# Block products' weights 32 bytes into longer slots, and a gap that moves the tensors behind it

## The chip, the core and the metric

One core of one Trainium2 chip runs the whole kernel as one program. The metric is device time of one execution in microseconds: the median over runs of the kernel. Before the change it is 1858.59 us in three runs (1858.54 to 1861.07).

## The reference

A trunk of two layers works on two requests of 256 tokens each, with shared weights, in float32. The tokens of both requests stand side by side: 512 columns of 1024 features. Each layer computes

```python
h = x + 0.5 * _swiglu(_rmsnorm(x, ffn1_norm[l]), ffn1_wg[l], ffn1_wu[l], ffn1_wd[l])
u = _rmsnorm(h, mix_norm[l])
p = u @ w_in[l]
ret = _retention(...)      # 4 heads of 128, forward and backward
dif = _diff_attn(...)      # 4 heads, differential attention with a relative bias
h = h + jnp.concatenate([ret, dif], axis=-1) @ w_out[l]
h = h + 0.5 * _swiglu(_rmsnorm(h, ffn2_norm[l]), ffn2_wg[l], ffn2_wu[l], ffn2_wd[l])
x = _rmsnorm(h, final_norm[l])
```

with `_swiglu(x, wg, wu, wd) = (silu(x @ wg) * (x @ wu)) @ wd` and 2816 hidden features. So there are four feed-forward networks (FFNs), two per layer, and they hold most of the multiplications.

## The kernel before, in words

Activations lie in SBUF with features on the 128 partitions and tokens along the free dimension. A weight matrix comes as units of 8 tiles of 128x128. A unit is loaded into a raw buffer (`raw`, `raw_x`), and split into a high and a low part of type float32r: ScalarE (ACT) writes the high part into `w_hi`, GpSimd (POOL) or VectorE (DVE) the difference into `w_lo`. Activations are split in the same way (`hg_hi`/`hg_lo`, `a_hi`/`a_lo`, `mix_*`, `s14_*`, `s2_*`). A product of two tiles is three matmuls that accumulate in one PSUM bank: weight high with activation high (L742), weight high with activation low (L743), weight low with activation high (L744), in the helper `three`. The program has a weight load for each of these matmuls.

There are six weight slots. Slots 0 to 3 are `w_hi[:, s]` and `w_lo[:, s]`; slots 4 and 5 are in further tensors `w_hi_x`, `w_lo_x`, which exist only in the FFNs. Each slot holds 8 tiles of 128 floats in a partition, 4096 bytes. `w_tiles(s, n, at_)` gives `n` tiles of a slot from tile `at_` on.

Whole units use a slot with 512 moving columns: all of attention's projections and output products (slots 0 to 3), two gate and up pairs at the start of an FFN (`CLASSIC_SLOT`), and the down products of the last chunk (`DOWN_SLOT`, which takes slots 4 and 5 too).

The rest of an FFN goes in 28 blocks. A block treats two units as a 2x2 matrix of half units, against the 2x2 of (halves of the features or hidden tiles) by (the two requests), and needs seven half-size products instead of eight, after Strassen and Winograd. So one block is 7 products of 4 tiles by 3 matmuls, 84 matmuls with 256 moving columns each. Block "t" makes a gate and up tile (20 of the 28), block "d" two down products (8 of them). Some products read `hg` or `a` directly, the others mixtures of two quarters: `mix_*` (mixtures of `hg`) in "t", `s14_*` and `s2_*` (gated sums) in "d". Even blocks use slots 0, 1, 2, odd ones 3, 4, 5 (`FAST_SLOTS`). TensorE's order in a block is p1, p6, p2, p5, p7, p4, p3; the two d blocks that open a chunk's down products have an order of their own. p1 and p2 use the first slot, p5 and p7 the second, p6, p4 and p3 the third. In "t", p1, p2, p4 and p3 read `hg` and p6, p5, p7 read `mix`; in "d", p1, p2, p7, p4 read `a` and p6, p5, p3 read `s14`, `s2`.

The order of all this is written out by hand for each engine, with semaphores: in `ffn` and `block_slot` of each engine. PE waits for a product's weights (POOL at L645, L663, L670, DVE at L1774) and for VectorE to have taken former products out of PSUM (`u` at L1800 and L1810 among them). Raw units are loaded by the SP queue.

SBUF tensors are placed one behind the other in a partition in the order of their declaration, each at the next multiple of 32 bytes. In the kernel before, `h` (at byte 1152) up to `blocks_r` all start at multiples of 64 bytes, since their sizes are. Behind them come small ones (`pr`, `eps`, ..., `lam`), and these leave off so that `raw_x` starts at byte 148320, 32 above a multiple of 64. Every further tensor has a multiple of 64 bytes again, so `raw_x`, `w_hi_x`, `w_lo_x`, `mix_*`, `up`, `s14_*` and `s2_*` start 32 above one. The tensors of attention (`decay`, `s1`, ..., `dkq`, `rkq`, `v`, `soft`) share that place in memory after the FFN's are given back, and start 32 above one too. All offsets within these tensors that a matmul reads from are multiples of 512 bytes.

Of the kernel before, what the change touches and what calls it, by code (L numbers as in the profile page):

```python
# [30 lines left out]
F32R = mybir.dt.float32r  # L31
# [4 lines left out]
P = 128  # L36
# [24 lines left out]
FAST = NF - CLASSIC  # L61
KH = KD // 2


# [131 lines left out]
def build(nc, x, w_gu, w_dn, w_p, w_o, par, lam_vec, table, one_hot, cossin, rel, ident_in, centre_in, y):  # L196
    with ExitStack() as ctx:
# [15 lines left out]
        raw = sb("raw", [P, RAW * UT * P])  # L213
        w_hi = sb("w_hi", [P, SLOTS, UT, P], F32R)
        w_lo = sb("w_lo", [P, SLOTS, UT, P], F32R)
        acc = sb("acc", [P, T])
# [19 lines left out]
        lg = sb("lg", [P, 8, 2 * HEADS])  # L236
        lam = sb("lam", [P, 6])


        with ExitStack() as ffn_only:  # L240
            def sb_ffn(name, shape, dt=F32):
                return ffn_only.enter_context(nc.sbuf_tensor(name, shape, dt))

            raw_x = sb_ffn("raw_x", [P, RAW * UT * P])
            w_hi_x = sb_ffn("w_hi_x", [P, 2, UT, P], F32R)
            w_lo_x = sb_ffn("w_lo_x", [P, 2, UT, P], F32R)
            mix_hi = sb_ffn("mix_hi", [P, 3, KH, SEQ], F32R)
# [365 lines left out]
        def _(pool):  # L613
# [45 lines left out]
            def lo_differences(l, f, b):  # L659
                pool.wait_ge(t13_hi, at(t13_hi, l, index(f, b) + 1))  # L660
                hi, lo_ = w_tiles(FAST_SLOTS[b % 2][1])
                both = raw_of(b)[:, :].rearrange("p (a b) -> p a b", a=2)[:, :, 0:KH * P]
                pool.tensor_tensor(columns(lo_).rearrange("p (a b) -> p a b", a=2), both,  # L663
                                   columns(hi).rearrange("p (a b) -> p a b", a=2).bitcast(F32),
                                   ALU.subtract).then_inc(t13_lo, 1)

            def lo_b22(l, f, b):
                pool.wait_ge(b22_hi, at(b22_hi, l, index(f, b) + 1))
                hi, lo_ = w_tiles(FAST_SLOTS[b % 2][2], KH, KH)
                pool.tensor_tensor(columns(lo_), raw_block(b, 1, 1), columns(hi).bitcast(F32),  # L670
                                   ALU.subtract).then_inc(b22_lo, 1)
# [66 lines left out]
        def _(pe):  # L738
            def three(out, w, m_hi, m_lo, first, last):

                hi, lo_ = w_tiles(w[0], 1, w[1])
                pe.matmul(out, hi[:, 0, :], m_hi, start=first, stop=False)  # L742
                pe.matmul(out, hi[:, 0, :], m_lo, start=False, stop=False)  # L743
                return pe.matmul(out, lo_[:, 0, :], m_hi, start=False, stop=last)  # L744
# [11 lines left out]
            def fresh_product(l, out, u, s, m_hi, m_lo):  # L756

                pe.wait_ge(hi_done, at(hi_done, l, u + 1))
                for k in range(UT):
                    pe.matmul(out, w_hi[:, s, k, :], m_hi[:, k, :], start=k == 0, stop=False)  # L760
                    pe.matmul(out, w_hi[:, s, k, :], m_lo[:, k, :], start=False, stop=False)
                pe.wait_ge(lo_done, at(lo_done, l, u + 1))
                for k in range(UT):
                    last = pe.matmul(out, w_lo[:, s, k, :], m_hi[:, k, :], start=False, stop=k == UT - 1)
                return last

            def first_two(l, outs, u, n0, done, between=None):
# [7 lines left out]
                for s in range(2):  # L775
                    pe.wait_ge(hi_done, at(hi_done, l, u + s + 1))
                    for k in range(EARLY):
                        if s == 0:
                            tile_hi(k)
                        pe.matmul(outs[s], w_hi[:, s, k, :], hg_hi[:, k, :], start=k == 0, stop=False)  # L780
                for s in range(2):
                    pe.wait_ge(lo_done, at(lo_done, l, u + s + 1))
                    for k in range(EARLY):
                        pe.matmul(outs[s], w_lo[:, s, k, :], hg_hi[:, k, :], start=False, stop=False)  # L784
                for s in range(2):
                    for k in range(EARLY):
                        if s == 0:
                            tile(k)
                        pe.matmul(outs[s], w_hi[:, s, k, :], hg_lo[:, k, :], start=False, stop=False)  # L789
                for s in range(2):  # L790
# [8 lines left out]
            def first_units():  # L799
# [3 lines left out]
                def high(s, k):  # L803
                    if s == 0:
                        pe.wait_ge(hg_hi_done, at(hg_hi_done, 0, k + 1))
                    pe.matmul(outs[s], w_hi[:, s, k, :], hg_hi[:, k, :], start=k == 0, stop=False)

                def moving_low(s, k):
                    if s == 0:
                        pe.wait_ge(hg_ready, at(hg_ready, 0, k + 1))  # L810
                    pe.matmul(outs[s], w_hi[:, s, k, :], hg_lo[:, k, :], start=False, stop=False)

                def weight_low(s, k, last=False):
                    return pe.matmul(outs[s], w_lo[:, s, k, :], hg_hi[:, k, :], start=False, stop=last)

# [20 lines left out]
                pe.wait_ge(hg_ready, at(hg_ready, 0, KD))  # L836
                pe.matmul(outs[0], w_hi[:, 0, KD - 1, :], hg_lo[:, KD - 1, :], start=False, stop=True).then_inc(gu_done, 1)
                moving_low(1, KD - 1)
# [352 lines left out]
        def _(act):  # L1191
# [27 lines left out]
            def hi_gate(l, f, b):  # L1219
                m = index(f, b)  # L1220
                raw_wait(l, ("t", m, 0))
                slot_free(l, f, b, 0, 4 if after_first_pair(b) else 2)
                act.activation(columns(w_tiles(FAST_SLOTS[b % 2][0])[0]), raw_tiles(RAW_AT["t", m, 0], UT),  # L1223
                               ACT.Copy).then_inc(g_hi, 1)

            def hi_differences(l, f, b):
                act.wait_ge(t13_done, at(t13_done, l, index(f, b) + 1))
                slot_free(l, f, b, 1, 5 if after_first_pair(b) else 7)
                both = raw_of(b)[:, :].rearrange("p (a b) -> p a b", a=2)[:, :, 0:KH * P]
                hi = columns(w_tiles(FAST_SLOTS[b % 2][1])[0]).rearrange("p (a b) -> p a b", a=2)  # L1230
                act.activation(hi, both, ACT.Copy).then_inc(t13_hi, 1)  # L1231

            def hi_b22(l, f, b):
                raw_wait(l, ("t", index(f, b), 1))
                slot_free(l, f, b, 2, 3)
                hi, _ = w_tiles(FAST_SLOTS[b % 2][2], KH, KH)
                act.activation(columns(hi), raw_block(b, 1, 1), ACT.Copy).then_inc(b22_hi, 1)
# [12 lines left out]
            def hi_t2(l, f, b):  # L1250
                act.wait_ge(t2_done, at(t2_done, l, index(f, b) + 1))
                slot_free(l, f, b, 2, 6 if after_first_pair(b) else 4)
                act.activation(columns(w_tiles(FAST_SLOTS[b % 2][2], KH)[0]), t_sum, ACT.Copy).then_inc(x_hi, 1)

            def hi_t4(l, f, b):
# [3 lines left out]
                act.wait_ge(p_done[q], at(p_done[q], l, m + 1))  # L1259
                act.activation(columns(w_tiles(t4_slot(b), KH)[0]), t_sum, ACT.Copy).then_inc(x_hi, 1)  # L1260

# [397 lines left out]
        def _(dve):  # L1659
# [111 lines left out]
            def lo_t(l, f, b, which):  # L1771
                dve.wait_ge(x_hi, at(x_hi, l, 2 * index(f, b) + which + 1))
                hi, lo_ = w_tiles(t4_slot(b) if which else FAST_SLOTS[b % 2][2], KH)
                dve.tensor_tensor(columns(lo_), t_sum, columns(hi).bitcast(F32), ALU.subtract).then_inc(x_lo, 1)  # L1774
# [558 lines left out]
```

## Time and profile before

| | |
|---|---|
| median of 3 runs | 1858.59 us |
| lowest, highest | 1858.54, 1861.07 us |
| span of the profiled execution | 1859.7 us |
| mean granted TensorE clock | 0.998 of full |
| PE busy, PEld busy | 1840.7 us, 1705.5 us |
| DVE, ACT, POOL busy | 1373.1, 1016.8, 1347.7 us |
| matmuls | 12668 |

The page gives the span of the profiled execution (from its first to its last instruction) and no time around it. Busy time of an engine is the time in which at least one of its instructions runs. For PE this hides how fast matmuls follow each other: one takes some 280 ns at 256 columns from its start to its end, but the next starts long before that. So for PE the distance between starts is read from the timeline or from counts in a stretch.

### The profile page before, as it was taken

How to read it: one execution, taken by the hardware profiler on the slowest of the kernel's cores; microseconds unless marked ns; L12 is line 12 of the kernel's file. 1: busy time of each engine (PE TensorE's matmuls, PEld its weight loads, DVE VectorE, ACT ScalarE, POOL GpSimd, SP SyncE). 2: the span in 40 equal slices, each digit the busy share in tenths (PEclk: the TensorE clock that was granted, in tenths of full speed). 3: DMA queues.
4: the chain of work that ended last, by engine and by line, in shares of the span. 5: the costliest groups of instructions: out<-in, count | busy, mean ns of one | idle time of the engine just before them, and what ended most of it. 6: DMA issues, size and time to landing. Idle time of an engine off the chain costs nothing. (4 is left out here: it accounts for less than half of the span.)

```text
span 1859.7 us, 33422 instructions
## 1 busy us (share of the span) xinstructions
PE 1840.7 (99%) x12668; PEld 1705.5 (92%) x12668; DVE 1373.1 (74%) x2396; ACT 1016.8 (55%) x1763; POOL 1347.7 (72%) x878
## 2 busy tenths in 40 slices
PE   8999999999999999999999999999999999999997
PEld 7999999887888999999889999998778889999995
DVE  6878887556755887887688888766577478878773
ACT  7655555456435655555575465555564266555452
POOL 5988897565445898988479998856544268988972
PEclk9999999999999999999999999999999999999999
DMA  3433233232223233323233333223222133323331
GB/s 138 154 112 126 96 126 114 77 103 70 69 68 113 73 110 114 106 100 108 75 113 137 100 106 114 105 78 114 79 68 73 53 113 115 106 100 114 105 106 63
DMA packets 55308, 186.71 MB, mean 100 GB/s; under 512 B 6472, under 2 KB 8264, under 8 KB 55148
## 3 DMA queue, kind: packets, MB, share of 16 engines
q1 hardware_dynamic: 53424, 181.61, 29.0%
q10 hardware_dynamic: 1724, 2.96, 0.5%
q8 instruction: 101, 1.65, 0.4%
q14 instruction: 59, 0.48, 0.1%
HBM read 182.44 MB, written 3.15 MB: 100 GB/s over the span
## 5 line engine op out<-in xcount | busy, mean ns | idle before, releaser
L742 PE MATMUL bank<-hg_hi,w_hi 128*128 128x256 f32 (+1 forms) x1396 | 445.2, 319 | 0.0
L743 PE MATMUL bank<-hg_lo,w_hi 128*128 128x256 f32 (+1 forms) x1396 | 441.4, 316 | 0.0
L744 PE MATMUL bank<-hg_hi,w_lo 128*128 128x256 f32 (+1 forms) x1396 | 441.2, 316 | 0.0
L636 POOL TENSOR_TENSOR w_lo<-raw,w_hi 128x512 fp32r<-128x512 f32 (+1 forms) x192 | 256.9, 1361 | 225.3 <-ACT w_hi L1206 225.2
L742 PEld LDWEIGHTS bank<-hg_hi,w_hi 128*128 128x128 f32 x1396 | 264.9, 190 | 19.9 <-issue 2.6
L744 PEld LDWEIGHTS bank<-hg_hi,w_lo 128*128 128x128 f32 x1396 | 265.1, 190 | 17.6
L743 PEld LDWEIGHTS bank<-hg_lo,w_hi 128*128 128x128 f32 x1396 | 265.1, 190 | 16.8
L1286 ACT ACTIVATE bank<-bank 128x512 f32<-128x512 f32 x88 | 51.1, 581 | 251.5 <-DVE bank L1831 251.5
L1206 ACT ACTIVATE w_hi<-raw 128x1024 fp32r<-128x1024 f32 (+1 forms) x96 | 98.0, 1025 | 120.2 <-PE bank L744 95.7
L663 POOL TENSOR_TENSOR w_lo<-raw_x,w_hi 128x1024 fp32r<-128x1024 f32 x56 | 134.9, 2410 | 26.3 <-ACT w_hi L1231 26.3
L645 POOL TENSOR_TENSOR w_lo<-raw_x,w_hi 128x1024 fp32r<-128x1024 f32 x56 | 136.1, 2430 | 17.0 <-ACT w_hi L1223 17.0
L663 POOL TENSOR_TENSOR w_lo_x<-raw,w_hi_x 128x1024 fp32r<-128x1024 f32 x56 | 135.0, 2410 | 14.1 <-ACT w_hi_x L1231 14.1
L645 POOL TENSOR_TENSOR w_lo<-raw,w_hi 128x1024 fp32r<-128x1024 f32 x56 | 136.5, 2438 | 2.7 <-ACT w_hi L1223 2.7
L742 PE MATMUL bank<-mix_hi,w_hi_x 128*128 128x256 f32 x480 | 135.5, 282 | 1.6 <-DVE u L1800 1.6
L742 PE MATMUL bank<-mix_hi,w_hi 128*128 128x256 f32 x480 | 135.2, 282 | 0.8 <-POOL w_lo L663 0.5
L744 PE MATMUL bank<-mix_hi,w_lo_x 128*128 128x256 f32 x480 | 135.3, 282 | 0.0
L743 PE MATMUL bank<-mix_lo,w_hi 128*128 128x256 f32 x480 | 135.1, 281 | 0.0
L743 PE MATMUL bank<-mix_lo,w_hi_x 128*128 128x256 f32 x480 | 134.9, 281 | 0.0
L744 PE MATMUL bank<-mix_hi,w_lo 128*128 128x256 f32 x480 | 134.5, 280 | 0.0
L742 PE MATMUL bank<-a_hi,w_hi 128*128 128x256 f32 (+1 forms) x448 | 134.0, 299 | 0.0
L743 PE MATMUL bank<-a_lo,w_hi 128*128 128x256 f32 (+1 forms) x448 | 133.5, 298 | 0.0
L744 PE MATMUL bank<-a_hi,w_lo 128*128 128x256 f32 (+1 forms) x448 | 133.5, 298 | 0.0
(342 smaller groups left out, 5831.5 us busy)
## 6 DMA issues: line engine op xcount, KB each, us to landing
raw<-in_w_gu SPq DMA_DIRECT2D x96, 512.0 KB, 4.0
raw_x<-in_w_gu SPq DMA_DIRECT2D x80, 512.0 KB, 4.2
raw<-in_w_p SPq DMA_DIRECT2D x56, 512.0 KB, 3.2
raw_x<-in_w_dn SPq DMA_DIRECT2D x32, 512.0 KB, 4.2
raw<-in_w_dn SPq DMA_DIRECT2D x32, 512.0 KB, 4.2
raw<-in_w_o SPq DMA_DIRECT2D x16, 512.0 KB, 3.3
raw_x<-in_w_dn SPq DMA_DIRECT2D x16, 384.0 KB, 4.0
raw<-in_w_dn SPq DMA_DIRECT2D x16, 384.0 KB, 3.4
```

The costliest lines, as they stand in the source:

```text
L636: ins = pool.tensor_tensor(columns(lo_[:, part, :]), source[:, part.start * P:part.stop * P], columns(hi[:, part, :]).bitcast(F32), ALU.su ...
L645: pool.tensor_tensor(columns(lo_), raw_tiles(RAW_AT["t", m, 0], UT), columns(hi).bitcast(F32), ALU.subtract).then_inc(g_lo, 1)
L663: pool.tensor_tensor(columns(lo_).rearrange("p (a b) -> p a b", a=2), both, columns(hi).rearrange("p (a b) -> p a b", a=2).bitcast(F32), A ...
L742: pe.matmul(out, hi[:, 0, :], m_hi, start=first, stop=False)
L743: pe.matmul(out, hi[:, 0, :], m_lo, start=False, stop=False)
L744: return pe.matmul(out, lo_[:, 0, :], m_hi, start=False, stop=last)
L1206: act.activation(columns(hi), raw_tiles(RAW_AT["e", e], TILES_OF[e]), ACT.Copy).then_inc(hi_done, 1)
L1286: act.activation(gated, gated, ACT.Silu).then_inc(silu_done, 1)
```

## The change: the diff and what it does

Each slot becomes a flat row of `SLOT` = 8 x 128 + 16 floats, 4160 bytes. Block products write and read their weights 8 floats (32 bytes) into the slot, through the new `block_tiles`; whole units still use it from its start, through `w_tiles`. A tensor `gap` of 8 floats (32 bytes), which nothing reads or writes, is declared behind `lam`. By the placing rule above, `raw_x` then starts at byte 148864, a multiple of 64, and all tensors behind it move likewise. No instruction is added or taken away, and none changes its shape.

```diff
+BLOCK_AT = 8
+SLOT = UT * P + 2 * BLOCK_AT
+GAP = 8
...
-        w_hi = sb("w_hi", [P, SLOTS, UT, P], F32R)
-        w_lo = sb("w_lo", [P, SLOTS, UT, P], F32R)
+        w_hi = sb("w_hi", [P, SLOTS, SLOT], F32R)
+        w_lo = sb("w_lo", [P, SLOTS, SLOT], F32R)
...
         lam = sb("lam", [P, 6])
+        sb("gap", [P, GAP])
...
-            w_hi_x = sb_ffn("w_hi_x", [P, 2, UT, P], F32R)
-            w_lo_x = sb_ffn("w_lo_x", [P, 2, UT, P], F32R)
+            w_hi_x = sb_ffn("w_hi_x", [P, 2, SLOT], F32R)
+            w_lo_x = sb_ffn("w_lo_x", [P, 2, SLOT], F32R)
...
-        def w_tiles(s, n=UT, at_=0):
+        def w_tiles(s, n=UT, at_=0, shift=0):
             hi, lo = (w_hi[:, s], w_lo[:, s]) if s < SLOTS else (w_hi_x[:, s - SLOTS], w_lo_x[:, s - SLOTS])
-            return hi[:, at_:at_ + n, :], lo[:, at_:at_ + n, :]
+            part = slice(shift + at_ * P, shift + (at_ + n) * P)
+            return hi[:, part].rearrange("p (a b) -> p a b", b=P), lo[:, part].rearrange("p (a b) -> p a b", b=P)
+
+        def block_tiles(s, n=UT, at_=0):
+            return w_tiles(s, n, at_, BLOCK_AT)
...
-                hi, lo_ = w_tiles(FAST_SLOTS[b % 2][0])
+                hi, lo_ = block_tiles(FAST_SLOTS[b % 2][0])
...
-            def three(out, w, m_hi, m_lo, first, last):
-                hi, lo_ = w_tiles(w[0], 1, w[1])
+            def three(out, w, m_hi, m_lo, first, last, tiles=w_tiles):
+                hi, lo_ = tiles(w[0], 1, w[1])
...
-                    last = three(prod[q] if out is None else out, (w, KH * half + k), m_hi[:, k, :], m_lo[:, k, :], k == 0, k == KH - 1)
+                    last = three(prod[q] if out is None else out, (w, KH * half + k), m_hi[:, k, :], m_lo[:, k, :],
+                                 k == 0, k == KH - 1, block_tiles)
```

The places that write block weights (`lo_gate`, `lo_differences`, `lo_b22` on POOL, `hi_gate`, `hi_differences`, `hi_b22`, `hi_t2`, `hi_t4` on ACT, `lo_t` on DVE) take `block_tiles` for `w_tiles` in the same way, and direct uses of `w_hi[:, s, k, :]` on PE become `w_hi[:, s, k_part(k)]` with the same addresses in the slot.

## Rows read from the trace of the kernel before

**Rows 1.** The page's first lines: busy us, share of the span, instructions.

```profile
span 1859.7 us, 33422 instructions
PE 1840.7 (99%) x12668; PEld 1705.5 (92%) x12668; DVE 1373.1 (74%) x2396; ACT 1016.8 (55%) x1763; POOL 1347.7 (72%) x878
```

**Rows 2.** Table by windows, stretches of block products: window, length, busy us, clock, DMA, GB/s.

```profile
core 0: us, PE busy (x) PEld busy (x) DVE busy (x) ACT busy (x) POOL busy (x), PEclk, DMA share, GB/s
...
660.00:880.00 220.00, 220.00 (x1852) 220.00 (x1852) 177.40 (x332) 120.00 (x200) 196.41 (x119) 1.00 0.32 108
...
1580.00:1790.00 210.00, 210.00 (x1769) 210.00 (x1768) 169.59 (x318) 115.29 (x191) 187.01 (x113) 1.00 0.31 106
```

**Rows 3.** Timeline of PE, t blocks 12 and 13: start us, duration us, instruction.

```profile
741.53 0.28 PE L742 MATMUL bank<-mix_hi,w_hi 128*128 128x256 f32 x1
...
742.95 0.28 PE L742 MATMUL bank<-mix_hi,w_hi 128*128 128x256 f32 x1
...
745.80 0.28 PE L742 MATMUL bank<-hg_hi,w_hi 128*128 128x256 f32 x1
...
747.24 0.28 PE L742 MATMUL bank<-hg_hi,w_hi 128*128 128x256 f32 x1
...
752.94 0.28 PE L742 MATMUL bank<-mix_hi,w_hi_x 128*128 128x256 f32 x1
...
754.38 0.28 PE L742 MATMUL bank<-hg_hi,w_hi_x 128*128 128x256 f32 x1
...
754.74 0.28 PE L742 MATMUL bank<-hg_hi,w_hi_x 128*128 128x256 f32 x1
...
757.21 0.28 PE L742 MATMUL bank<-hg_hi,w_hi 128*128 128x256 f32 x1
```

**Rows 4.** Timeline of PE, d block 9: first matmuls of p7, p4 and p3.

```profile
713.00 0.28 PE L742 MATMUL bank<-a_hi,w_hi_x 128*128 128x256 f32 x1
...
714.42 0.28 PE L742 MATMUL bank<-a_hi,w_hi_x 128*128 128x256 f32 x1
...
715.83 0.28 PE L742 MATMUL bank<-s_h,w_hi_x 128*128 128x256 f32 x1
```

**Rows 5.** Timeline of PE, last down products with 512 columns, slots 3, then 4.

```profile
908.45 0.39 PE L742 MATMUL pair<-a_hi,w_hi 128*128 128x512 f32 x1
...
913.21 0.39 PE L742 MATMUL pair<-a_hi,w_hi 128*128 128x512 f32 x1
...
913.90 0.39 PE L742 MATMUL pair<-a_hi,w_hi_x 128*128 128x512 f32 x1
...
921.60 0.40 PE L742 MATMUL pair<-a_hi,w_hi_x 128*128 128x512 f32 x1
```

**Rows 6.** Groups by line and form, PE, 512 columns from slots 4 and 5.

```profile
L742 PE MATMUL pair<-a_hi,w_hi_x 128*128 128x512 f32 x72 | 28.4, 395 | 0.0
...
L742 PE MATMUL pair<-hg_hi,w_hi_x 128*128 128x512 f32 x32 | 12.7, 398 | 0.0
```

**Rows 7.** The page's groups: POOL's low parts; busy us, mean ns, idle before.

```profile
L663 POOL TENSOR_TENSOR w_lo<-raw_x,w_hi 128x1024 fp32r<-128x1024 f32 x56 | 134.9, 2410 | 26.3 <-ACT w_hi L1231 26.3
...
L663 POOL TENSOR_TENSOR w_lo_x<-raw,w_hi_x 128x1024 fp32r<-128x1024 f32 x56 | 135.0, 2410 | 14.1 <-ACT w_hi_x L1231 14.1
```

**Rows 8.** Timeline of POOL and DVE, low parts for block 13.

```profile
744.76 2.42 POOL L663 TENSOR_TENSOR w_lo_x<-raw,w_hi_x 128x1024 fp32r<-128x1024 f32 x1
...
750.98 0.69 DVE L1774 TENSOR_TENSOR w_lo_x<-bank,w_hi_x 128x512 fp32r<-128x512 f32 x1 [0.32 <-ACT w_hi_x L1260]
```

**Rows 9.** PE's waits, longest in total first: us, times, longest us.

```profile
PE bank L742 <- DVE u L1800: 2.4, 3, 1.1
PE bank L806 <- ACT hg_hi L1631: 2.3, 1, 2.3
```

**Rows 10.** Instructions of lines 854 and 868: duration ns min/median/max, first, last.

```profile
L854 PE MATMUL bank<-s_h,ones_r x6: 397/397/501, 363.7 to 1521.0; 128*128 128x512 f32 x6
...
L868 PE MATMUL bank<-a_hi,blocks_r x16: 389/389/390, 385.9 to 1373.9; 128*128 128x512 f32 x16
```

More of the change, by code:

```diff
@@ L660, in lo_differences @@
                 pool.wait_ge(t13_hi, at(t13_hi, l, index(f, b) + 1))
-                hi, lo_ = w_tiles(FAST_SLOTS[b % 2][1])
+                hi, lo_ = block_tiles(FAST_SLOTS[b % 2][1])
                 both = raw_of(b)[:, :].rearrange("p (a b) -> p a b", a=2)[:, :, 0:KH * P]
@@ L668, in lo_b22 @@
                 pool.wait_ge(b22_hi, at(b22_hi, l, index(f, b) + 1))
-                hi, lo_ = w_tiles(FAST_SLOTS[b % 2][2], KH, KH)
+                hi, lo_ = block_tiles(FAST_SLOTS[b % 2][2], KH, KH)
                 pool.tensor_tensor(columns(lo_), raw_block(b, 1, 1), columns(hi).bitcast(F32),
@@ L738, in _, with k_part @@
         def _(pe):
-            def three(out, w, m_hi, m_lo, first, last):
-                hi, lo_ = w_tiles(w[0], 1, w[1])
+            def k_part(k):
+                return slice(k * P, (k + 1) * P)
+            def three(out, w, m_hi, m_lo, first, last, tiles=w_tiles):
+                hi, lo_ = tiles(w[0], 1, w[1])
                 pe.matmul(out, hi[:, 0, :], m_hi, start=first, stop=False)
@@ L759, in fresh_product @@
                 for k in range(UT):
-                    pe.matmul(out, w_hi[:, s, k, :], m_hi[:, k, :], start=k == 0, stop=False)
-                    pe.matmul(out, w_hi[:, s, k, :], m_lo[:, k, :], start=False, stop=False)
+                    pe.matmul(out, w_hi[:, s, k_part(k)], m_hi[:, k, :], start=k == 0, stop=False)
+                    pe.matmul(out, w_hi[:, s, k_part(k)], m_lo[:, k, :], start=False, stop=False)
                 pe.wait_ge(lo_done, at(lo_done, l, u + 1))
                 for k in range(UT):
-                    last = pe.matmul(out, w_lo[:, s, k, :], m_hi[:, k, :], start=False, stop=k == UT - 1)
+                    last = pe.matmul(out, w_lo[:, s, k_part(k)], m_hi[:, k, :], start=False, stop=k == UT - 1)
                 return last
@@ L779, in first_two @@
                             tile_hi(k)
-                        pe.matmul(outs[s], w_hi[:, s, k, :], hg_hi[:, k, :], start=k == 0, stop=False)
+                        pe.matmul(outs[s], w_hi[:, s, k_part(k)], hg_hi[:, k, :], start=k == 0, stop=False)
                 for s in range(2):
@@ L783, in first_two @@
                     for k in range(EARLY):
-                        pe.matmul(outs[s], w_lo[:, s, k, :], hg_hi[:, k, :], start=False, stop=False)
+                        pe.matmul(outs[s], w_lo[:, s, k_part(k)], hg_hi[:, k, :], start=False, stop=False)
                 for s in range(2):
@@ L788, in first_two @@
                             tile(k)
-                        pe.matmul(outs[s], w_hi[:, s, k, :], hg_lo[:, k, :], start=False, stop=False)
+                        pe.matmul(outs[s], w_hi[:, s, k_part(k)], hg_lo[:, k, :], start=False, stop=False)
                 for s in range(2):
@@ L805, in high @@
                         pe.wait_ge(hg_hi_done, at(hg_hi_done, 0, k + 1))
-                    pe.matmul(outs[s], w_hi[:, s, k, :], hg_hi[:, k, :], start=k == 0, stop=False)
+                    pe.matmul(outs[s], w_hi[:, s, k_part(k)], hg_hi[:, k, :], start=k == 0, stop=False)
                 def moving_low(s, k):
@@ L810, in moving_low @@
                         pe.wait_ge(hg_ready, at(hg_ready, 0, k + 1))
-                    pe.matmul(outs[s], w_hi[:, s, k, :], hg_lo[:, k, :], start=False, stop=False)
+                    pe.matmul(outs[s], w_hi[:, s, k_part(k)], hg_lo[:, k, :], start=False, stop=False)
                 def weight_low(s, k, last=False):
-                    return pe.matmul(outs[s], w_lo[:, s, k, :], hg_hi[:, k, :], start=False, stop=last)
+                    return pe.matmul(outs[s], w_lo[:, s, k_part(k)], hg_hi[:, k, :], start=False, stop=last)
                 pe.wait_ge(hi_done, at(hi_done, 0, 1))
@@ L836, in first_units @@
                 pe.wait_ge(hg_ready, at(hg_ready, 0, KD))
-                pe.matmul(outs[0], w_hi[:, 0, KD - 1, :], hg_lo[:, KD - 1, :], start=False, stop=True).then_inc(gu_done, 1)
+                pe.matmul(outs[0], w_hi[:, 0, k_part(KD - 1)], hg_lo[:, KD - 1, :], start=False, stop=True).then_inc(gu_done, 1)
                 moving_low(1, KD - 1)
@@ L1222, in hi_gate @@
                 slot_free(l, f, b, 0, 4 if after_first_pair(b) else 2)
-                act.activation(columns(w_tiles(FAST_SLOTS[b % 2][0])[0]), raw_tiles(RAW_AT["t", m, 0], UT),
+                act.activation(columns(block_tiles(FAST_SLOTS[b % 2][0])[0]), raw_tiles(RAW_AT["t", m, 0], UT),
                                ACT.Copy).then_inc(g_hi, 1)
@@ L1229, in hi_differences @@
                 both = raw_of(b)[:, :].rearrange("p (a b) -> p a b", a=2)[:, :, 0:KH * P]
-                hi = columns(w_tiles(FAST_SLOTS[b % 2][1])[0]).rearrange("p (a b) -> p a b", a=2)
+                hi = columns(block_tiles(FAST_SLOTS[b % 2][1])[0]).rearrange("p (a b) -> p a b", a=2)
                 act.activation(hi, both, ACT.Copy).then_inc(t13_hi, 1)
@@ L1235, in hi_b22 @@
                 slot_free(l, f, b, 2, 3)
-                hi, _ = w_tiles(FAST_SLOTS[b % 2][2], KH, KH)
+                hi, _ = block_tiles(FAST_SLOTS[b % 2][2], KH, KH)
                 act.activation(columns(hi), raw_block(b, 1, 1), ACT.Copy).then_inc(b22_hi, 1)
@@ L1252, in hi_t2 @@
                 slot_free(l, f, b, 2, 6 if after_first_pair(b) else 4)
-                act.activation(columns(w_tiles(FAST_SLOTS[b % 2][2], KH)[0]), t_sum, ACT.Copy).then_inc(x_hi, 1)
+                act.activation(columns(block_tiles(FAST_SLOTS[b % 2][2], KH)[0]), t_sum, ACT.Copy).then_inc(x_hi, 1)
             def hi_t4(l, f, b):
@@ L1259, in hi_t4 @@
                 act.wait_ge(p_done[q], at(p_done[q], l, m + 1))
-                act.activation(columns(w_tiles(t4_slot(b), KH)[0]), t_sum, ACT.Copy).then_inc(x_hi, 1)
+                act.activation(columns(block_tiles(t4_slot(b), KH)[0]), t_sum, ACT.Copy).then_inc(x_hi, 1)
             def copy_p1(l, f, b):
@@ L1772, in lo_t @@
                 dve.wait_ge(x_hi, at(x_hi, l, 2 * index(f, b) + which + 1))
-                hi, lo_ = w_tiles(t4_slot(b) if which else FAST_SLOTS[b % 2][2], KH)
+                hi, lo_ = block_tiles(t4_slot(b) if which else FAST_SLOTS[b % 2][2], KH)
                 dve.tensor_tensor(columns(lo_), t_sum, columns(hi).bitcast(F32), ALU.subtract).then_inc(x_lo, 1)
```

## The prediction

> **What bounds the kernel now.** I began with the page's first part: TensorE (PE) is busy for 99% of the span, the weight loads (PEld) beside it for 92%, POOL and VectorE for about 72 to 74% [rows 1]. The table by windows then shows what PE does in the stages of block products. In two stretches of 220 and 210 us it is busy without a gap, and it starts 1852 and 1769 matmuls in them [rows 2]. That is 220/1852 = 118.8 ns from one start to the next, and 210/1769 = 118.7 ns. (A matmul's own duration, 0.28 us, is latency; they overlap, so the distance of starts is what costs.) There are 4 FFNs x 28 blocks x 7 products x 12 = 9408 such matmuls, each with 256 moving columns and its own weight load: 1118 us of the 1859.7. Everything else in these stretches is hidden as long as it keeps up. So the question is whether the change alters the distance of starts.
>
> The change moves data and adds no instruction; the operations keep their shapes. Only addresses within a partition move. Before it, every tensor from `h` to `blocks_r`, with `w_hi` and `w_lo` (slots 0 to 3), starts at a multiple of 64 bytes; everything behind `lam` (`raw_x`, slots 4 and 5, the mixtures `mix_*`, the gated sums `s14_*`, `s2_*`) starts 32 bytes above one. The trace of before thus already holds all four pairings of moving operand (M) and weights (W), named by their distance above a multiple of 64. I took them from the timeline as distances between the first matmuls of successive products; a product has 12.
> - M 0, W 0 (`hg` with slot 2): 747.24 - 745.80 = 1.44 us, 120.0 ns each [rows 3].
> - M 32, W 32 (`mix` with slot 4): 754.38 - 752.94 = 1.44 us, 120.0 ns [rows 3].
> - M 32, W 0 (`mix` with slot 1): 742.95 - 741.53 = 1.42 us, 118.3 ns [rows 3].
> - M 0, W 32 (`hg` with slot 5): 21 matmuls from 754.74 to 757.21, 2.47 us, 117.6 ns [rows 3].
>
> Could it be the product's place or its PSUM bank? The product that starts at 752.94 is the fifth of an odd block; the same step four blocks earlier, in a block of down products, with `a` (M 0) for `mix` (M 32) and the same slot and bank, takes 714.42 - 713.00 = 1.42 us where the one with `mix` took 1.44, and the next one 715.83 - 714.42 = 1.41 [rows 3, 4]. So equal phases cost 120.0 ns, and unequal ones about 2 ns less.
>
> With 512 columns it is the other way round. At M 0, W 0, 21 matmuls take 913.21 - 908.45 = 4.76 us, 226.7 ns each; at M 0, W 32, 33 take 921.60 - 913.90 = 7.70 us, 233.3 ns [rows 5].
>
> **The change part by part.** *Block weights at +8 elements, slots lengthened by 64 bytes, a gap of 32 bytes behind `lam`.* A slot is then 4160 = 65 x 64 bytes, so every slot starts at a multiple of 64 and every block product's weights 32 above one. The gap brings `raw_x` and all behind it from 32 to 0. All 9408 block matmuls become M 0, W 32. At 117.6 ns they gain 118.8 - 117.6 = 1.2 ns each, 11.3 us.
> One thing isn't in the trace: slots 0, 2 and 4 put the block weights 32 above a multiple of 128, slots 1, 3 and 5 96 above; the pairing read above had 96 (slots 4 and 5 of before). If 128 bytes matter, the nearest row for the other half is M 32, W 0 with its 118.3 ns (`mix` stands 96 above a multiple of 128, so the weights lie 32 beyond it). Its ends, from the rows of both widths: 117.6 at best, 120.0 plus the 6.6 ns of the 512-column case at worst. I take between 117.6 and 118.3 for that half, the values nearest to it: half of the matmuls, 4704, gain 1.2 ns and the others about 0.9: 5.6 + 4.2 = 9.8 us.
>
> *Slots 4 and 5 for whole units.* The last down products and one of the opening units use them with 512 columns: 3 x (72 + 32) = 312 matmuls [rows 6], which go from 233.3 to 226.7 ns: 2.1 us gained.
>
> *Attention.* Its tensors that share the place behind `lam` go from 32 to 0 together; its projections (slots 0 to 3, `hg`) stay M 0, W 0. Those of slots 1 and 3 come to stand 64 above a multiple of 128, which no row shows; the ends are 226.7 and 233.3 ns. I take 226.7, since all that these rows show goes by 32 against 64.
>
> *ScalarE, VectorE, POOL, DMA.* They write and read the moved tensors in the same shapes. POOL takes 2410 ns for the weights' low part whether it goes from a tensor 32 above to one at 0 or from 0 to 32 [rows 7]. I cost this at nothing.
>
> *What is late next.* The gain holds only where PE is ahead of nobody. POOL has 196.4 of 220 us busy, VectorE 177.4 [rows 2]; with a block shorter by 1% POOL comes to some 90%. The weights are early: in the block read above POOL begins slot 4's low part at 744.76, for 2.42 us, so it is ready at 747.18, and PE uses it from 751.52 (12 matmuls before 752.94, M 32, W 32); VectorE's low part of slot 5 is ready at 751.67 for 754.38 [rows 3, 8]. Covers of 2.7 us and more against 0.1 us a block. But where PE already waits, what it saves ahead of the wait is lost. PE's list of waits has few: 2.4 us in 3 waits for VectorE's `u` (L1800) [rows 9]. They stand in the first two blocks of the first FFN and at the first paired down products of layer 1's first FFN, where VectorE has extra work. What is lost is the saving of the blocks before: about two blocks in each of four FFNs (4 x 2 x 84 x 1.2 ns = 0.8 us) and six more in that one (0.6 us), 1.4 us in all.
>
> **Sum**: -9.8 - 2.1 + 1.4 = -10.5 us. The profiled execution has a span of 1859.7 us, 1.1 above the median of 1858.6 and within the three runs (1858.5 to 1861.1); nothing is shown of what lies around it, so I take the difference from the median: 1848.1, rounded to 1848.0.
>
> **Rivals.**
> 1. *Not the phase, but the place* (the change does nothing to the rate). In the trace of before, "32 above" and "behind `lam`" are the same tensors. If the 2 ns come from operands on two sides of a border in SBUF, the changed kernel keeps every pairing: 1858.6. Against it: `ones_r` with `s2` (M 32) takes 397 ns, its neighbour `blocks_r` with `a` (M 0) 389 at the same 512 columns [rows 10], which phase explains as it stands; a border would have to lie exactly at `lam`. The Trainium skill, page "SBUF — State Buffer", section "Who interferes with whom", would give this result too: it has two independent read ports for PE, moving operand and weights, and says that PE never waits on anyone. By that rule addresses of one could not slow the other, and 1858.6 would stand. The rows at 120.0 and 117.6 ns for one shape disagree with it.
> 2. *The phase counts in 128 bytes, without a gain at 32.* Slots 0, 2, 4 then go at 120.0 (+1.2 on 4704, 5.6 us lost), the others gain 5.6, slots 4 and 5 at 512 columns 2.1: 1856.5 or a little more. For it: only one residue was seen with M 0. Against: M 32, W 0 has the same distance and is fast.
> 3. *The feeders hold it back.* If VectorE's chain through `u` binds in every block rather than in a few, half of the gain goes: 1853. For it: the waits on L1800. Against: the covers above.
> 4. *Slower: misaligned weights cost at 256 columns what they cost at 512.* Place: block products from slots 0, 2 and 4, at 32 above a multiple of 128. Price: 6.6 ns on 4704 matmuls, 31 us, less 5.6 and 2.1 gained elsewhere: 1882. It decides from the first block on. It needs the unseen residue to act like 512 columns although slots 4 and 5 with the same form gain.
>
> **How the numbers follow.** Forecast 0.74, feeders 0.06, place 0.07, 128 bytes without gain 0.07, slower 0.06. The forecast's own range is 1844 (all at 117.6, 118.8 - 117.6 on 9408 and 2.1, nothing lost: -13.4, to 1845.2, with 1 us of spread between runs) to 1851 (all of the unseen half at 118.3 or worse and 3 us lost in waits). Stretched to the cases of rivals 2 and 3 it ends at 1857, which leaves out rival 1 and 4. About 0.2%, 3.7 us, is what a measurement can tell from no change: faster than that 0.74 + 0.06 = 0.80, within it 0.14, slower 0.06.
>
> **What would show it.** In the timeline of after, each product of 12 takes 1.41 to 1.42 us whatever it reads, none 1.44; a block 9.88 to 9.91 instead of 9.98; the two window rows give about 117.7 ns a matmul. Down products from slots 4 and 5 go at 226.7. POOL's and VectorE's durations stay. If even blocks' products from slots 0 and 2 differ from those of slot 1, the 128-byte question is answered. The prediction is wrong if 1.44 us remains with M 0, W 32, or if PE's waits grow by several us.

## The result: slightly slower, and the profile after

| | before | after |
|---|---|---|
| median, us | 1858.54 | 1862.87 |
| lowest to highest | 1858.38 to 1861.18 | 1862.66 to 1864.19 |
| ratio to before, 95% interval | | 1.0021 [1.0014, 1.0027] |
| span of the traced execution, us | 1859.7 | 1862.4 |
| the four block stretches, first to last matmul start, us | 1124.2 | 1120.7 |
| all the rest of the span, us | 735.5 | 741.7 |
| of the rest: ahead of the first block, us | 36.4 | 34.9 |
| of the rest: behind the first block's start, us | 699.1 | 706.8 |
| mean distance of starts within blocks (distances under 150 ns), ns | 118.87 | 118.39 |

The forecast was 1848.0, faster; the kernel became 4.3 us slower (13 runs each). An execution's time lies 1.8 us above its span, so the traced execution of before is one of 1861.4 us, at the top of its runs, and that of after one of 1864.2. The traces therefore differ by 2.7 us where the medians differ by 4.3. The lines of the table below the span are worked out from the starts in the timeline: a block stretch is one FFN's 28 blocks, 2352 matmuls.

Most of the missing 1.6 us lie ahead of the first block, which starts at 36.36 us in the trace of before and at 34.93 in that of after (at 33.4 to 34.5 in the traces of the seven whole kernels further down). PE waits there for its first activations, 2.3 us before [rows 9] and 1.6 after. In the trace of before the granted clock was also lower for a while: 0.86 and 0.72 of full in two windows, 0.50 (the lower level, 1.2 GHz) between 11 and 14 us, while it was 1.00 in those windows of after. Before, then after, columns of [rows 2]:

```profile
8.00:12.00 4.00, 2.46 (x11) 2.07 (x11) 3.49 (x4) 4.00 (x7) 1.63 (x2) 0.86 1.02 358
12.00:16.00 4.00, 4.00 (x16) 3.31 (x15) 4.00 (x6) 4.00 (x7) 2.22 (x2) 0.72 0.18 58
...
8.00:12.00 4.00, 2.53 (x14) 2.16 (x15) 3.54 (x4) 4.00 (x8) 1.56 (x2) 1.00 1.01 365
12.00:16.00 4.00, 4.00 (x20) 3.28 (x19) 4.00 (x6) 4.00 (x7) 2.28 (x2) 1.00 0.14 48
```

So the traces are best compared from the first block on: there the difference is 4.2 us, as between the medians.

The blocks did gain, 3.5 us. The rest behind the first block's start lost 7.7. Both show in rows. The page's first lines of after (answering to [rows 1]):

```profile
span 1862.4 us, 33422 instructions
...
PE 1844.1 (99%) x12668; PEld 1702.3 (91%) x12668; DVE 1380.0 (74%) x2396; ACT 1016.8 (55%) x1763; POOL 1345.9 (72%) x878
```

The table by windows of after, the two stretches of [rows 2], same columns:

```profile
660.00:880.00 220.00, 220.00 (x1858) 219.90 (x1858) 177.62 (x333) 120.80 (x201) 197.11 (x118) 1.00 0.32 108
1580.00:1790.00 210.00, 210.00 (x1775) 209.90 (x1774) 170.22 (x319) 115.06 (x192) 188.33 (x114) 1.00 0.33 110
```

Six more matmuls in each stretch: 220/1858 = 118.4 ns and 210/1775 = 118.3, where 117.7 was expected. The clock is 1.00 of full in both, and POOL and VectorE are as busy as before. The timeline of after, PE, blocks 12 and 13 (answering to [rows 3]) shows which products gained; these are first matmuls of products, with start and duration in us:

```profile
738.18 0.29 PE L754 MATMUL bank<-hg_hi,w_hi 128*128 128x256 f32 x1
739.60 0.28 PE L754 MATMUL bank<-mix_hi,w_hi 128*128 128x256 f32 x1
...
745.30 0.28 PE L754 MATMUL bank<-hg_hi,w_hi 128*128 128x256 f32 x1
746.74 0.28 PE L754 MATMUL bank<-hg_hi,w_hi 128*128 128x256 f32 x1
748.17 0.28 PE L754 MATMUL bank<-hg_hi,w_hi 128*128 128x256 f32 x1
749.57 0.28 PE L754 MATMUL bank<-mix_hi,w_hi_x 128*128 128x256 f32 x1
...
752.39 0.28 PE L754 MATMUL bank<-mix_hi,w_hi_x 128*128 128x256 f32 x1
753.81 0.29 PE L754 MATMUL bank<-mix_hi,w_hi_x 128*128 128x256 f32 x1
...
758.07 0.28 PE L754 MATMUL bank<-hg_hi,w_hi 128*128 128x256 f32 x1
...
908.17 0.39 PE L754 MATMUL pair<-a_hi,w_hi 128*128 128x512 f32 x1
...
913.06 0.40 PE L754 MATMUL pair<-a_hi,w_hi 128*128 128x512 f32 x1
...
914.46 0.39 PE L754 MATMUL pair<-a_hi,w_hi_x 128*128 128x512 f32 x1
...
922.09 0.40 PE L754 MATMUL pair<-a_hi,w_hi_x 128*128 128x512 f32 x1
```

A product from slot 0 takes 739.60 - 738.18 = 1.42 us, from slot 2 1.44 and 1.43, from slot 3 1.40, from slot 4 1.42. The operands stand 32 bytes apart modulo 64 in all of them, and the slots differ all the same. The whole gain is in the odd blocks, which use slots 3 to 5: block 13 takes 758.07 - 748.17 = 9.90 us, where it took 757.21 - 747.24 = 9.97 [rows 3], while the 56 even blocks together take 562.0 us before and 561.9 after. The last four rows answer to [rows 5]: 21 matmuls with 512 columns from slot 3 take 4.89 us, 232.9 ns each, where they took 226.7; the 33 behind them, slot 4, take 7.63 us, 231.2 ns instead of 233.3. In attention it is alike. A projection unit (24 matmuls, the first starts of its first and last tile) before:

```profile
386.40 0.39 PE L742 MATMUL bank<-hg_hi,w_hi 128*128 128x512 f32 x1
...
391.16 0.39 PE L742 MATMUL bank<-hg_hi,w_hi 128*128 128x512 f32 x1
```

and after:

```profile
384.91 0.39 PE L754 MATMUL bank<-hg_hi,w_hi 128*128 128x512 f32 x1
...
389.81 0.40 PE L754 MATMUL bank<-hg_hi,w_hi 128*128 128x512 f32 x1
```

21 matmuls in 4.76 us (226.7 ns) before, in 4.90 (233.3) after. That is where 7.1 of the 7.7 us lie. From the last matmul of the blocks of layer 0's first FFN to the first of its second FFN's, with attention between them, before and then after:

```profile
319.14 0.28 PE L744 MATMUL bank<-hg_hi,w_lo_x 128*128 128x256 f32 x1
...
617.24 0.28 PE L742 MATMUL bank<-hg_hi,w_hi 128*128 128x256 f32 x1
...
316.83 0.28 PE L756 MATMUL bank<-hg_hi,w_lo_x 128*128 128x256 f32 x1
...
618.51 0.28 PE L754 MATMUL bank<-hg_hi,w_hi 128*128 128x256 f32 x1
```

298.10 us became 301.68; in layer 1 it is 298.13 and 301.66. Of the two longest entries in PE's list of waits (us, times, longest), the first hardly moved from [rows 9] and the second, at the start, fell:

```profile
PE bank L754 <- DVE u L1813: 2.4, 3, 1.2
PE bank L818 <- ACT hg_hi L1644: 1.6, 1, 1.6
```

So nothing waits for anything new. Matmuls of whole units follow each other more slowly.

### The profile page after: what moved, and what is told of

It is laid out like the page before. It is cut to its first block and busy times, and to the rows that moved or that the text cites. A ratio compares the mean times of both kernels' runs of the same rounds, so it can differ in the third digit from the quotient of the medians.

```text
span 1862.4 us, 33422 instructions
## 1 busy us (share of the span) xinstructions
PE 1844.1 (99%) x12668; PEld 1702.3 (91%) x12668; DVE 1380.0 (74%) x2396; ACT 1016.8 (55%) x1763; POOL 1345.9 (72%) x878
## 5 line engine op out<-in xcount | busy, mean ns | idle before, releaser
L645 POOL TENSOR_TENSOR w_lo<-raw,w_hi 128x512 fp32r<-128x512 f32 (+1 forms) x192 | 256.1, 1356 | 227.8 <-ACT w_hi L1219 227.6
```

Source lines behind the costliest of these rows:

```text
L645: ins = pool.tensor_tensor(columns(lo_[:, part, :]), source[:, part.start * P:part.stop * P], columns(hi[:, part, :]).bitcast(F32), ALU.su ...
```

## The experiments

Two theories stood at first. **A**: what counts is the distance of weights and moving operand over a longer period than 64 bytes; 512 was taken at first. The new slot length of 4160 = 16 x 256 + 64 bytes then puts each slot at a distance of its own. **B**: 64 bytes as in the prediction. **C** is the border at `lam`, rival 1. "Distance" is the weights' address less that of the moving operand.

**Scan of the distance by itself** (e1_scan). Streams of the products' form, with the weights' address stepped by 32 bytes and no other engine busy beside them. `FINE` goes from 0 to 992 bytes in steps of 32, with high and low weights alike; `COARSE` from 0 to 448 in steps of 64, for high and low weights apart.

```diff
+            for d in FINE:
+                fine_256(d, d, 8)
+            for d in FINE:
+                fine_512(d, d, 2)
+            for d in COARSE:
+                for e in COARSE:
+                    last = coarse_256(d, e, 5)
```

> The trunk is left out: the kernel only runs streams of matmuls in the pattern of the block products (weight high with moving high, weight high with moving low, weight low with moving high) on copies of x, without waits, and returns x. The distance from moving operand to weights goes from 0 to 992 bytes in steps of 32, first 32 sections of 96 matmuls with 256 columns, then 32 sections of 48 with 512 columns; then 64 sections of 60 with 256 columns where the distance of the high and of the low weights go separately through 0, 64, ..., 448. In the traces of before and after, the distances were 0, 224 and 288 bytes modulo 512 (before) and eight others (after). Theory A (distance counts modulo 512): 120.0 ns at 0 and 512, 117.6 at 224 and 736, the second half repeats the first; 512 columns 226.7 at 0 and 512 alone and 229 to 235 at others. Rival B (modulo 64, as the prediction had it): the sections alternate between 120.0 and 117.6 ns, and between 226.7 and 233.3. Rival C (sides of a border at lam, no phase): all sections 120.0 and 226.7, since all tensors lie below it.

Measured, ns from start to start: with 256 columns 120.0, 118.3, 117.8, 117.3, 120.0, 119.9, 117.8, 117.8 for 0, 32, ... 224 bytes, and the same again from 256, 512 and 768 on (the very first section opens with some 20 distances of 213 ns and then goes at 120.0). With 512 columns 226.7, 233.4, 233.4, 234.3, 232.4, 233.4, 228.8, 233.3, again repeated. With high and low weights apart, 64 bytes for the high and 192 for the low gives 113.3, at all four places of the grid that are the same modulo 256; the others give 116.6 to 120.0. The timeline of this scan, PE: first a distance of 256, then 288, then 512 columns at 0 and 32, then 64/192; 72, 72, 24, 24 and 36 matmuls lie between the two rows of each pair:

```profile
112.09 0.28 PE L58 MATMUL pa<-m_hi,w_hi 128*128 128x256 f32 x1
...
120.73 0.28 PE L58 MATMUL pa<-m_hi,w_hi 128*128 128x256 f32 x1
...
123.59 0.28 PE L58 MATMUL pb<-m_hi,w_hi 128*128 128x256 f32 x1
...
132.11 0.28 PE L58 MATMUL pb<-m_hi,w_hi 128*128 128x256 f32 x1
...
386.73 0.39 PE L69 MATMUL pa<-m_hi,w_hi 128*128 128x512 f32 x1
...
392.17 0.39 PE L69 MATMUL pa<-m_hi,w_hi 128*128 128x512 f32 x1
...
397.69 0.40 PE L69 MATMUL pb<-m_hi,w_hi 128*128 128x512 f32 x1
...
403.29 0.40 PE L69 MATMUL pb<-m_hi,w_hi 128*128 128x512 f32 x1
...
819.83 0.28 PE L80 MATMUL pb<-m_hi,w_hi 128*128 128x256 f32 x1
...
823.91 0.28 PE L80 MATMUL pb<-m_hi,w_hi 128*128 128x256 f32 x1
```

8.64 us / 72 = 120.0; 8.52 / 72 = 118.3; 5.44 / 24 = 226.7; 5.60 / 24 = 233.3; 4.08 / 36 = 113.3. The period is 256 bytes, half of what A had: B falls, and C cannot explain a scan within one tensor. It also reads the prediction's own rows anew. `hg` and slots 0 to 3 were at distance 0. `mix` with slot 1 was at 32 (118.3 there and here), `hg` with slot 5 at 224 (117.6 and 117.8), the 512 columns of slot 4 at 224 (233.3 and 233.3). What the prediction called "M 0, W 32" was 224, and in the changed kernel only slot 3 stands at 224 for high and low weights, with slot 5's low weights.

**The gap alone, at two sizes** (e2_gap32, e3_gap288).

```diff
         lam = sb("lam", [P, 6])
+        sb("gap", [P, 8])
```

(72 floats for 8 in the second.)

> The kernel before with the gap of 32 bytes alone; slots stay 4096 bytes and block weights stay at the slots' start. All tensors then start at multiples of 64; those behind lam come to lie 256 bytes modulo 512 from the others (224 before). Theory A (modulo 512): pairings across lam stay unequal, their products keep 116.5 to 119.5 ns, pairings within one side keep 120.0: 1855 to 1862 us. Rival B (modulo 64): every block matmul goes at 120.0 (+1.2 ns on 9408, 11.3 us), slots 4 and 5 with 512 columns at 226.7 (-2.1): 1867.8 us. Rival C (border at lam): nothing changes, 1858.6.

> The kernel before with a gap of 288 bytes behind lam: every operand of a block product then has the same address modulo 512. Theory A (modulo 512) and rival B (modulo 64; 288 is 4.5 times 64): all block matmuls 120.0 ns (+11.3 us), 512 columns from slots 4 and 5 at 226.7 instead of 233.3 (-2.1): 1867.8 us. Rival C (border at lam): every pairing keeps its pitch, 1858.6.

Measured: 1865.40 us, ratio 1.0037 [1.0025, 1.0050], and 1865.41, 1.0038 [1.0024, 1.0051]. A gap of 32 leaves the tensors behind `lam` 256 bytes off those ahead of it (modulo 512), one of 288 leaves nothing between them, and the two are equal: 256 counts as 0. Every matmul in blocks then goes at 119.99 ns. Block 13 in the timeline of the first, from its first matmul to the next block's:

```profile
748.19 0.28 PE L743 MATMUL bank<-hg_hi,w_hi 128*128 128x256 f32 x1
...
758.27 0.28 PE L743 MATMUL bank<-hg_hi,w_hi 128*128 128x256 f32 x1
```

10.08 us, 84 x 120.0. The block stretches add up to 1133.7 us (+9.5). The rest is 730.0 (-5.5); 3.0 of that lie ahead of the first block, which starts at 33.4 us here, and behind its start the rest is 696.6 (-2.5, where 2.1 was forecast for slots 4 and 5). So A with 512 bytes missed the first kernel (1855 to 1862), and the forecast of 1867.8, B's for both and A's for the second, was 2.4 too high: the blocks lost 9.5 us for 11.3, and the rest gained 0.4 more. C, which has no change at 1858.6, falls here. A with 256 bytes and B say the same of these two kernels; the scan and the next run tell them apart.

**Longer slots alone** (e4_longer): the change without shift and gap.

```diff
-        sb("gap", [P, GAP])
...
-            return w_tiles(s, n, at_, BLOCK_AT)
+            return w_tiles(s, n, at_, 0)
```

> The change without its shift and without its gap: slots of 4160 bytes, block weights at the slots' start. Theory A (modulo 512): the slots come to lie 0, 64, 128, 192 bytes (high) and 256, 320, 384, 448 (low) from the moving operand, so whole units with 512 columns lose their 226.7 ns as in the changed kernel: 229 to 234, +6 to +8 us in all; block products somewhere between 117 and 119.5, -8 to 0 us: 1857 to 1867. Rival B (modulo 64): every slot is still a multiple of 64, 226.7 stays, block products as before: 1858.6 within 1 us.

1861.04 us, ratio 1.0017 [1.0009, 1.0026]. This lies in A's interval and excludes B: slots moved by multiples of 64 bytes alone make the kernel 2.5 us slower. In its traced execution blocks take 1118.6 us, the rest 740.3 (706.7 behind the first block's start, 7.6 more than before), the same two opposite movements as in the changed kernel. The blocks are 2.1 us faster here than in the changed kernel: what they gained came from the slots' length, and the shift of 32 bytes with the gap, on which the prediction rested, took some of it back.

**A grid for high and low weights, with the low activations moved too** (e5_grid).

```diff
+            for d_m in MOVING:
+                for d in FINE:
+                    for e in FINE:
+                        stream(SEQ, 4, d, e, d_m, 3)
```

> The trunk is left out, as in the first scan: streams of matmuls alone. That scan repeated every 256 bytes (120.0 ns at 0 and 256, 117.3 to 120.0 between; 512 columns 226.7 at 0 and 256, 228.8 at 192, 232 to 234 elsewhere), and its last part showed 113.3 ns where the high weights lie 64 and the low ones 192 bytes from the moving operand. This one has 256 sections with 256 columns (36 matmuls each) and 256 with 512 columns (24 each): high weights, then low weights at 0, 32, ..., 224, and the low moving operand 0, 64, 128, 192 bytes from the high one. Theory D (three distances modulo 256 set the rate, nothing else): with equal moving phases, (0,0) gives 120.0 and (64,192) 113.3; the values at the changed kernel's distances, averaged over its slots (high/low 32/32, 96/96, 160/160, 224/224, 32/160, 96/224), come to its 118.4 within 0.5; a shift of everything by the same amount changes nothing. Rival E (only the distance of the high weights counts, as long as the two moving phases agree): each row of the grid is constant within 0.5 ns. For 512 columns D leaves open whether any pair is below 226.7.

The pairs of the changed kernel's slots: 32/32 118.2, 96/96 117.4, 160/160 120.0, 224/224 116.7, 32/160 118.2, 96/224 117.8 ns. Their mean is 118.05 (118.17 if each slot counts by its products, 2, 2 and 3 in a block), and 118.39 was measured in its blocks; that is near, with 0.2 to 0.3 ns over. That the high weights' distance alone sets the pace (E) fell: rows of the grid vary by up to 5.4 ns (64 for the high weights: 113.4 to 118.8). Nothing went below 113.3, and nothing below 115 with the low activations moved; with 512 columns 0/0 is the lowest, 226.7, with everything else at 227.7 and above. D's "nothing else" fell too: some pairs that gave one value in the first scan gave another here (224/224: 117.8 and 116.7; 192/128: 117.8 and 115.7). Equal addresses and 64/192 came out alike each time.

**The changed kernel with attention's units put back to distance 0** (e9_att0): they are written 192, 128 and 64 bytes further into slots 1 to 3, and two waits on `out_done` go one unit later.

```diff
+        def mixer_tiles(s, n=UT, at_=0):
+            start = (0, 1088, 2112, 3136)[s] + at_ * P
+            return tuple(w[:, :, :].rearrange("p a b -> p (a b)")[:, start:start + n * P].rearrange("p (a b) -> p a b", b=P)
+                         for w in (w_hi, w_lo))
...
-                        last = product(proj[t], s, hg_hi, hg_lo, KD)
+                        last = product(proj[t], s, hg_hi, hg_lo, KD, of=mixer_tiles)
```

> The changed kernel, except that attention's projections and output products (1728 of the 2688 matmuls with 512 columns) find their weights at distance 0 modulo 256 in every slot (slots 1 to 3 are written 192, 128 and 64 bytes further for them). Blocks and the FFNs' whole units stay as the change has them. Theory A (the loss comes from whole units that the slots' new length of 4160 bytes moved off distance 0; 231.3 ns in the trace of the changed kernel, 227.5 before): 1728 x 3.8 = 6.6 us back, less up to 1 us for writers that wait one unit longer: 1856.3 to 1857.5 after 1862.9, so a little faster than before, by what the blocks gained. Rival G (the loss lies elsewhere, in waits or the blocks): 1862 to 1864.

1856.78 us, ratio to before 0.9986 [0.9977, 0.9995]. This is what A gave, and it is the experiment that settles the sign: blocks stay as the change has them (1120.8 us, 118.39 ns), and the rest falls from 741.7 to 734.2. Behind the first block's start it falls from 706.8 to 700.2, 6.6 us as forecast; the stretch across attention is 298.4 us again. The 1.1 us that remain over before's 699.1 go with the FFNs' whole units, which stand as the change has them (those into `pair` from slots 0 to 3 follow each other in 230.8 ns, before in 227.6). The same projection unit as above, in this kernel:

```profile
383.27 0.39 PE L762 MATMUL bank<-hg_hi,w_hi 128*128 128x512 f32 x1
...
388.04 0.39 PE L762 MATMUL bank<-hg_hi,w_hi 128*128 128x512 f32 x1
```

4.77 us for 21, back from 4.90.

**All products at 64 and 192** (e6_placed), **attention at 0** (e7_placed2), **all FFN weights at 96** (e8_placed96). These start from the kernel before, with slots of 4096 bytes; the diff is that of the first.

```diff
+        sb("gap0", [P, 16])
         w_hi = sb("w_hi", [P, SLOTS, UT, P], F32R)
+        sb("gap1", [P, 32])
         w_lo = sb("w_lo", [P, SLOTS, UT, P], F32R)
...
         lam = sb("lam", [P, 6])
+        sb("gap2", [P, 40])
...
             w_hi_x = sb_ffn("w_hi_x", [P, 2, UT, P], F32R)
+            sb_ffn("gap3", [P, 32])
             w_lo_x = sb_ffn("w_lo_x", [P, 2, UT, P], F32R)
+            sb_ffn("gap4", [P, 16])
```

The second reads and writes attention's units through a view of `w_hi`, `w_lo` that starts 16 floats away, and two waits on `out_done` go one unit later. The third is the second with 24 floats for both parts of the FFNs' weights, and gaps to suit.

> The kernel before with gaps alone, slots of 4096 bytes as there: in every product the high weights lie 64 bytes above the activations modulo 256, the low weights 192 bytes. Theory A (the distance modulo 256 sets the pitch, and the pair counts): 9408 block matmuls go from 118.8 to the 113.3 ns of the scan, -51.7 us; 2376 matmuls with 512 columns from slots 0 to 3 go from 226.7 to 231.8, +12.1, and 312 from slots 4 and 5 from 233.3 to 231.8, -0.5: 1818.4 us, up to 1824 with what waits take back. Rival B (modulo 64, as in the prediction): all pairings equal, 120.0 ns and 226.7 ns: 1867.8. Rival F (the feeders bind once blocks take 9.52 us; POOL would be 94% busy in them): 1835 to 1845, with PE waiting on POOL's low parts.

> As the kernel with every product at 64 and 192, but attention's projections and output products (1728 matmuls with 512 columns) read their weights at distance 0, written 64 bytes away from where the FFNs have them in the slot; some writers then wait for one more unit to be done. Theory A: 1728 x 5.1 ns = 8.8 us less than the other: 1809.6, up to 1815 with waits. Rival B: 1867.8, no difference between the two. Rival F: 8.8 us less than the other all the same, since attention's stretches are PE's, so 1826 to 1836.

> As the kernel with attention at distance 0, but high and low weights of the FFNs both 96 bytes above the activations modulo 256. Theory A: block matmuls 118.8 to 117.3 ns, -13.9 us; 648 matmuls with 512 columns of the FFNs from 226.7 to 234.3, +4.9, and 312 from 233.3 to 234.3, +0.3: 1849.8, to 1852 with waits. So 40 us slower than the kernel with 64 and 192 though its feeders are the same. Rival B (modulo 64: 96 is 32): 117.6 and 233.3, 1858.5 - 11.3 + 4.3 = 1851.5, the fastest of the three by 16 us.

| | median, us | ratio [95%] | blocks, us | pace in blocks, ns | rest, us |
|---|---|---|---|---|---|
| 64/192 everywhere | 1830.89 | 0.9849 [0.9836, 0.9862] | 1086.7 | 113.42 | 742.3 |
| 64/192, attention at 0 | 1823.70 | 0.9812 [0.9799, 0.9825] | 1086.6 | 113.42 | 735.3 |
| 96/96, attention at 0 | 1858.00 | 0.9993 [0.9985, 1.0002] | 1118.1 | 118.09 | 736.3 |

The second is the fastest kernel of this study, 34.9 us below before, with the same instructions in the same order. The first two came out between A's and F's ranges, the third above A's. A's pace came out as in the scan (113.3 forecast, 113.42 measured), and so did the cost at 512 columns (7.0 us between the first two in the rest, 7.9 behind the first block's start, 8.8 forecast). But 37.5 of the 51.7 us came out in the blocks, and rival F has a share in that. PE's waits in the first of the three, and its window (PE, PEld, DVE, ACT and POOL busy):

```profile
660.00:880.00 220.00, 218.59 (x1919) 217.89 (x1919) 181.42 (x341) 123.26 (x204) 201.29 (x123) 1.00 0.33 113
...
PE bank L747 <- DVE u L1805: 8.5, 12, 1.4
```

12 waits for VectorE's `u`, 8.5 us, for 3 and 2.4 before. What distances of 150 ns and more hold beyond one pace goes from 6.4 to 20.1 us: those 13.7 are the missing gain, and 6.1 of them are the longer waits for `u`. Another 2.0 are waits for other results of VectorE (low parts, 2.8 us for 0.8 before); the list does not name the rest. The waits for `u` stand at p6 of the second block of an FFN and at p6 of the second of the two down blocks that open a chunk (1.1 us each in the first chunk). F's size (1835 to 1845) and its culprit (POOL's low parts, 0.6 us in one wait) were wrong; the waits that grew are for VectorE, above all for its taking products out of PSUM. A single block shows the pace by itself, block 13 of the same kernel:

```profile
735.55 0.28 PE L747 MATMUL bank<-hg_hi,w_hi 128*128 128x256 f32 x1
...
745.07 0.28 PE L747 MATMUL bank<-hg_hi,w_hi 128*128 128x256 f32 x1
```

9.52 us, 84 x 113.3; it was 9.97 before.

The kernel at 96 was expected at 1849.8 to 1852 and fell short: 118.1 ns in its blocks for the 117.3 of the scan. Its runs spread from 1854.4 to 1861.8, 7.4 us, where those of every other kernel here lie within 3.3. At unequal distances the pace can depend on what went before: the scan, with no other engine beside it, gave 120.0 ns for 128/128 in its first part and 118.7 in its last. So the history of the stream is enough to move it. Why is open, and so is how much of the 0.8 ns at 96 comes from history and how much from other traffic in the kernel.

## Why the prediction was wrong, step by step

- **What bounds the kernel: right.** PE's distance of starts sets the time of the blocks. [Rows 2] and the same windows after agree with the stretches, and at 64/192 the same instructions gain 1.5 and 1.9%.
- **Reading the phase modulo 64 bytes: wrong, and the step that failed.** The rows of before hold only three distances modulo 256 (0, 32 and 224), and the prediction gave them two names, equal and unequal. So "all 9408 become M 0, W 32 at 117.6" took the pace of 224 for 32, 96 and 160 as well. At the changed kernel's distances the scan has 118.3, 117.3, 119.9 and 117.8 ns for slots 0 to 3, where the prediction had 117.6 to 118.3 for all.
- **Blocks: right in sign, too large.** Forecast 9.8 us. Measured (118.87 - 118.39) x 9408 = 4.5, less 1.0 more in long distances: 3.5. Slot 2 (160) had least to gain, slot 3 (224) most, and even blocks gained nothing. The 117.6 itself was read from 21 matmuls; the 24 from 754.38 to 757.21 in [rows 3] take 2.83 us, 117.9 ns. The question left open for the 128-byte residue was the right one, but its ends stood around the wrong value.
- **Attention and whole units: wrong sign.** "No row shows" 64, 128 and 192 with 512 columns, and the prediction took 226.7 from its two ends, since all that its rows showed went by 32 against 64. In after, matmuls of whole units follow each other in 231.3 ns for 228.2 (the mean of all distances under 260 ns in unbroken stretches of 20 matmuls or more); 3.0 ns x 2688 is some 8 us lost, and 7.7 show behind the first block's start. The far end of the step, 6.6 ns on the 864 of attention's 1728 matmuls that use slots 1 and 3, is 5.7 us; it was named and then left out of the range, and the FFNs' whole units from slots 0 to 3 and attention's slot 2 were not seen to move at all.
- **Slots 4 and 5 at 226.7: wrong.** 231.2 in the rows above, 231.4 over all such units for 233.2, a gain of 0.6 us for 2.1. The length of the slot puts the low weights of slot 4 at 128, and slot 5 at 64 and 192; the grid has 230.9 and 231.9 ns for these pairs.
- **Other engines at nothing, waits little changed: right** (POOL 1345.9 us for 1347.7, 2.4 us for `u` before and after), so rival 3 fell. The place of the waits was misread without effect: in before one stands in the second block of the first FFN and two in layer 1's first FFN, in its second block and at p6 of its eighth.
- **Sum.** Blocks -3.5, the rest behind the first block's start +7.7: +4.2, where -10.5 was forecast. Of the 14.7 us between them 6.3 are the blocks' and 9.8 the rest's, which was forecast 2.1 faster; the 1.4 that the forecast had put down for waits goes off again, since the blocks' 3.5 hold what was lost in them.
- **The rivals.** Rival 1 fell in the scan and with the gap alone. Rival 2 guessed that more than 64 bytes count and kept a gain of 2.1 at slots 4 and 5; it was nearest in idea. Rival 4 had the price (some 6 ns at a residue not seen), but at 256 columns; it was paid at 512.

The prediction cited the Trainium skill, page "SBUF — State Buffer", section "Who interferes with whom", by which moving operand and weights have read ports of their own and PE never waits on anyone. The scan disagrees for one stream with nothing beside it: 113.3 to 120.0 ns by the distances of addresses alone.

## What to carry to other kernels

When PE's pace depends on addresses, measure it over a full period before reasoning from a residue: three distances in a trace can carry two names that do not hold for the fourth. A padding that shifts one access also sets the stride of everything in that tensor; list what every user of it, here the whole units, comes to stand at. In this kernel gaps alone that put the high weights 64 and the low weights 192 bytes above the activations modulo 256 gave 1.5%; with equal addresses for attention's 512 columns as well it was 1.9%, without an instruction added.

## What the runs showed of the hardware

- The distance of starts of float32r matmuls, each with its own weight load, depends on the distance of weights and moving operand modulo 256 bytes: at 256 columns 113.3 ns (64 for the high, 192 for the low weights) against 120.0 (equal), at 512 columns 226.7 (equal) against 234.3 (96). The best place at one width is a poor one at the other: 64/192 gives 231.8 at 512 columns.
- Equal addresses and 64/192 gave the same pace wherever a whole stream had them (120.0 in the scan, 119.99 in the kernel with a gap alone; 113.3 and 113.42). Some other distances gave paces up to 2.1 ns apart in different streams (192/128: 117.8 and 115.7). The kernel with 96 varied by 7.4 us from run to run, the others by 3.3 at most.
- The Trainium skill, page "TensorE: Matmul & The Clock Gate", section "Back-to-back issue gap", has N/2.4 + 2.5 ns for an isolated gap with N columns: 109.2 at 256 and 215.8 at 512, an estimate from its formula. Here each matmul has its own weight load, and no stream came lower than 113.3 and 226.7.
